# Modulation vectors from raw fp32 weight blocks held stationary, with silu(c) as the moving operand

## What is computed

```python
shift, scale, gate = jnp.split(jax.nn.silu(c) @ wm + bm, 3, axis=-1)        # wm: 2048 x 6144
shift_c, scale_c = jnp.split(jax.nn.silu(c_ctx) @ wm[:, :2 * D_MODEL] + bm[:2 * D_MODEL], 2, axis=-1)
hx = rmsnorm(h, norm_g[layer]) * (1.0 + scale[:, None]) + shift[:, None]
hc = rmsnorm(ctx, norm_g[layer]) * (1.0 + scale_c) + shift_c
proj = hx @ wi                                                              # queries, keys, values, gates of two attentions
...
oa = diff_attention(qa, ka, va, ka_c, va_c, ...)                            # attention "a"
ob = neighbourhood_attention(qb, kb, vb, kb_c, vb_c, rpb_l, rows)           # attention "b"
mixed = jnp.concatenate([oa, ob], axis=-1) @ w_out[layer]
h = h + gate[:, None] * mixed
return rmsnorm(h, final_g)
```

## Time and profile before

| | us |
|---|---|
| median of 3 runs | 3143.16 (3136.03 to 3157.03) |
| the profiled execution, its own time | 3152.64 |
| span of its trace | 3150.9 |
| first stage, start of the span to the first matmul of the projection a | 223.5 |
| attend_a, from its first POOL instruction to the first slab of projection b | 507.1 to 600.8 |
| projection b, queries and the first head of keys | 600.8 to 659.9 |

### The profile page before, as it was taken

One profiled execution on the slowest core, in us unless ns is written; L12 is line 12 of the kernel. 1 busy time (PEld: TensorE's weight loads), 2 busy tenths in 40 slices (PEclk: granted clock), 3 DMA queues, 4 the chain that ended last, 5 costly groups with the idle time before them and its releaser, 6 DMA issues. The chain is left out here.

```text
span 3150.9 us, 52606 instructions
## 1 busy us (share of the span) xinstructions
PE 2911.8 (92%) x15816; PEld 2475.9 (79%) x15816; DVE 1801.5 (57%) x3346; ACT 1450.7 (46%) x2697; POOL 621.6 (20%) x488
## 2 busy tenths in 40 slices
PE   6879997799979699987799999999999999999996
PEld 4658785688857599965699998888888888888885
DVE  5784325532345665455678785555555666666666
ACT  6663234432344344443344445555554555555553
POOL 0030001210000000000000077878761211111110
PEclk9999998899989899986999999999999999999998
DMA  6873237332424255442454577777776666666663
GB/s 237 287 232 131 89 105 289 87 122 94 144 82 170 103 186 184 165 155 87 153 186 168 177 183 175 186 187 187 187 193 238 216 218 220 217 214 217 220 212 133
DMA packets 182877, 554.08 MB, mean 176 GB/s; under 512 B 53664, under 2 KB 53696, under 8 KB 179488
## 3 DMA queue, kind: packets, MB, share of 16 engines
q1 hardware_dynamic: 137696, 517.03, 48.8%
q0 software_dynamic: 44544, 32.10, 5.9%
q10 hardware_dynamic: 576, 4.19, 0.3%
HBM read 532.13 MB, written 21.10 MB: 176 GB/s over the span
## 5 line engine op out<-in xcount | busy, mean ns | idle before, releaser
L153 DVE TENSOR_TENSOR w_lo<-raw,w_hi 128x512 fp32r<-128x512 f32 x1888 | 1306.0, 717 | 934.2 <-ACT w_hi L146 918.3
L146 ACT ACTIVATE w_hi<-raw 128x512 fp32r<-128x512 f32 x1888 | 1143.1, 629 | 938.7 <-PE PS L164 845.8
L1745 PE MATMUL PS<-h,w_hi 128*128 128x512 f32 x1504 | 533.1, 400 | 2.0 <-DVE w_lo L153 2.0
L1658 POOL DMA_INDIRECT g_dram<-gt,spot x256 | 414.2, 1618 | 458.4 <-DVE gt L1986 348.7
L1747 PE MATMUL PS<-h,w_lo 128*128 128x256 f32 x1504 | 423.1, 281 | 0.0
L162 PE MATMUL PS<-w_hi,wj_hi 128*128 128x512 f32 x1024 | 399.2, 390 | 4.9 <-DVE wj_lo L1794 4.9
L163 PE MATMUL PS<-w_lo,wj_hi 128*128 128x512 f32 x1024 | 398.8, 389 | 0.0
L164 PE MATMUL PS<-w_hi,wj_lo 128*128 128x512 f32 x1024 | 398.8, 389 | 0.0
L1745 PEld LDWEIGHTS PS<-h,w_hi 128*128 128x128 f32 x1504 | 283.4, 188 | 73.2 <-DVE w_lo L153 2.4
L1747 PEld LDWEIGHTS PS<-h,w_lo 128*128 128x128 f32 x1504 | 284.8, 189 | 0.0
L162 PE MATMUL PS<-h,w_hi 128*128 128x256 f32 x800 | 228.8, 286 | 5.0 <-DVE w_lo L153 2.9
(11 more groups left out here) (327 smaller groups left out, 4418.6 us busy)
## 6 DMA issues: line engine op xcount, KB each, us to landing
raw<-in_u_s SPq DMA_DIRECT2D x256, 512.0 KB
raw<-in_v SPq DMA_DIRECT2D x256, 512.0 KB
raw<-in_w_in_s SPq DMA_DIRECT2D x112, 512.0 KB
raw<-in_w_mod_s SPq DMA_DIRECT2D x96, 512.0 KB
raw<-in_w_in_a SPq DMA_DIRECT2D x64, 512.0 KB
raw<-in_w_in_b SPq DMA_DIRECT2D x64, 512.0 KB
raw<-in_w_out_s SPq DMA_DIRECT2D x64, 512.0 KB
g_dram<-h_buf SPq DMA_DIRECT2D x1, 16384.0 KB, 42.8
```

What stands on the lines that cost most here:

```text
L146: act.activation(w_hi[m % 2][:, half], raw[:, m % NRAW, half], ACT.Copy).then_inc(hi_ready, 1)
L153: dve.tensor_tensor(w_lo[m % 2][:, half], raw[:, m % NRAW, half], w_hi[m % 2][:, half].bitcast(F), ALU.subtract).then_inc(lo_ready, 1)
L1658: pool.indirect_dma_start(g_dram, bass.IndirectOffsetOnAxis(spot[:, t, h, k:k + 1], 0), gt[:, t, h, k:k + 1], None, compute_op=ALU.add).th ...
L1745: pe.matmul(PS[:, 6 + j % 2, :], w_hi[m % 2][:, c], h_both[:, kk, :, :].rearrange("p a t -> p (a t)"), start=(kk == 0), stop=False)
```

## The change

shift and scale are now made block by block of 128 features (k = 0 to 15). A slab of w_mod_s holds 8 blocks of 128x128 of w_mod, and two slabs (`half`) hold the 16 input blocks of one output block. Each 128x128 block of `raw`, in plain fp32 and neither rounded nor split, is the stationary side of one matmul with csilu (2 columns: c and c_ctx) as the moving side; 16 of these add up into two columns of PSUM, in which the result already lies as a column, so that mod_row and its transposes are gone. PE itself counts the slab as used (`lo_ready` by 2). Slabs 0 to 15 come before the transposes of x, 16 to 63 after them, and then 32 slabs of the gate (`w_gate_s`) in the same form. DVE adds the bias, makes the factor and applies both to xT for each k; ACT rounds and POOL subtracts as before. The counters that ACT, DVE and PE no longer raise one by one are raised once at the start.

Beside that, clearing h_buf and writing it over g_dram moves from attend_a (POOL, SP) into projection b, on POOL's queue: after the bias loads and ahead of the mask, as 8 DMAs of 2 MB. And attend_a transposes into one PSUM bank where it had two.

```diff
-N_MOD, N_WIN_A, N_WIN_B, ... = 96, 64, 64, ...
+N_MOD, N_WIN_A, N_GATE, N_WIN_B, ... = 64, 64, 32, 64, ...
 (sync, first stage)
                         load_slabs(sp, src_mod, 0, NRAW, N_MOD)
+                        load_slabs(sp, src_gate, base["gate"], 0, NRAW)
+                        load_slabs(sp, src_gate, base["gate"], NRAW, N_GATE)
                         load_slabs(sp, src_a, base["a"], 0, NRAW)
 (scalar)
-                        act.activation(cc_hi[:, :, :], cc[...], ACT.Copy).then_inc(cc_round, 1)
-                        round_slab(act, None, 0)
...
-                                round_slab(act, None, 8 * u + g + 1)
...
+                        act.sem_inc(hi_ready, 2 * (N_MOD + N_GATE))
+                        for t in range(4):
+                            act.wait_ge(x_in[t], 16)
...
+                        for k in range(KT):
+                            if k == KT - 1:
+                                round_slab(act, None, base["a"])
+                            act.wait_ge(affine, k + 1)
+                            act.activation(x_hi[:, k, :], xT[:, k, :], ACT.Copy).then_inc(x_round, 1)
 (vector)
-                            for g in range(16):
-                                split_slab(dve, q * 16, 16 + g + 1)
-                            for u in range(2):
-                                add_bias(q, 2 + u)
...
+                        for k in range(KT):
+                            dve.wait_ge(lo_ready, 8 * (k + 1))
+                            i = dve.tensor_tensor(mk[:, k, :, :], PS[:, 4 + k % 4, 0:4].rearrange("p (a w) -> p a w", a=2),
+                                                  biases[:, k, :][:, :, None].broadcast_to([P, 2, 2]), ALU.add)
+                            i.then_inc(mod_out, 1)
...
+                            for w in range(2):
+                                part = xT[:, k, w * T:(w + 1) * T]
+                                i = dve.tensor_scalar(part, part, ab[:, k, w:w + 1], mk[:, k, 0, w:w + 1], ALU.mult, ALU.add)
+                            i.then_inc(affine, 1)
+                        dve.wait_ge(lo_ready, 2 * base["a"])
+                        dve.tensor_tensor(gateT[:, :, :], PS[:, 1, 0:2 * KT]..., ALU.add)
+                        split_slab(dve, None, base["a"])
 (tensor)
-                                        mm3(pe, PS[:, 6 + u, :], (cc_hi[:, kk, :], cc_lo[:, kk, :]),
-                                            (w_hi[m % 2][:, c], w_lo[m % 2][:, c]), kk == 0, kk == KT - 1).then_inc(multiplied, 1)
...
+                        def shift_and_scale(k):
+                            if k >= 4:
+                                pe.wait_ge(mod_out, k - 3)
+                            for a in range(2):
+                                for half in range(2):
+                                    m = 4 * k + 2 * a + half
+                                    raw_wait(pe, (None, m))
+                                    for j in range(8):
+                                        last = pe.matmul(PS[:, 4 + k % 4, 2 * a:2 * a + 2], raw[:, m % NRAW, j * P:(j + 1) * P],
+                                                         csilu[:, 8 * half + j, :], start=(half == 0 and j == 0),
+                                                         stop=(half == 1 and j == 7))
+                                    last.then_inc(lo_ready, 2)
+                        for k in range(4):
+                            shift_and_scale(k)
                         pe.wait_ge(small, 64)
-                        mod_transposes(None, 0)
                         for k in range(KT):
...
                                 last = pe.transpose(PS[:, k % 4, t * P:(t + 1) * P], xs[:, t, k * P:(k + 1) * P], ident)
-                        with loop(pe, 5) as q:
-                            mod_pair(q, 1)
-                            mod_transposes(q, 1)
+                        for k in range(4, KT):
+                            shift_and_scale(k)
+                        pe.wait_ge(tr_outv, KT // 2)
+                        for e in range(KT):
+                            for half in range(2):
+                                m = base["gate"] + 2 * e + half
+                                raw_wait(pe, (None, m))
+                                for j in range(8):
+                                    last = pe.matmul(PS[:, 1, 2 * e:2 * e + 2], raw[:, m % NRAW, j * P:(j + 1) * P], ...)
+                                last.then_inc(lo_ready, 2)
 (attend_a)
-                        sp.wait_ge(blank, 1)
-                        sp.dma_start(g_blank, h_buf[...].broadcast_to([P, 8, TT * D])).then_inc(g_blanked, 16)
...
-                        pool.memset(h_buf[:, :, :], 0.0).then_inc(blank, 1)
...
-                                last = pe.transpose(PS[:, 4 + t, c * P:(c + 1) * P], at_[:, t, c * P:(c + 1) * P], ident)
+                                last = pe.transpose(PS[:, 4, c * P:(c + 1) * P], at_[:, t, c * P:(c + 1) * P], ident)
 (projection b, gpsimd)
                             pool.wait_ge(bias_in, 64)
+                            pool.memset(h_buf[:, :, :], 0.0).then_inc(blank, 1)
+                            pool.wait_ge(blank, 1)
+                            for c in range(8):
+                                pool.dma_start(g_blank[:, c, :], h_buf[...]).then_inc(g_blanked, 16)
```

More of the change, by code:

```diff
@@ L237, in peer_block_kernel @@
         at = 0
-        for name, n in (("mod", N_MOD), ("a", N_WIN_A), ("b", N_WIN_B), ("out", N_OUT), ("in2", N_WIN2),
+        for name, n in (("mod", N_MOD), ("gate", N_GATE), ("a", N_WIN_A), ("b", N_WIN_B), ("out", N_OUT), ("in2", N_WIN2),
                         ("out2", N_OUT2), ("wq", N_WQ), ("u", N_U), ("v", N_V)):
@@ L441, in _ @@
                         dve.wait_ge(small, 64)
-                        for u in range(2):
-                            add_bias(None, u)
                         for k in range(1, KT, 2):
@@ L500, in mod_transposes @@
-                        def mod_transposes(reg, pair):
-                            for u in range(2):
-                                tile = 2 * pair + u
-                                pe.wait_ge(row_in, tile + 1 if reg is None else reg * 2 + (tile + 1))
-                                if pair:
-                                    pe.wait_ge(mod_out, tile - 1 if reg is None else reg * 2 + (tile - 1))
-                                for c in range(4):
-                                    last = pe.transpose(PS[:, 4 + u, c * P:(c + 1) * P], mod_row[:, u, c * P:(c + 1) * P], ident)
-                                last.then_inc(mod_tr, 1)
-                                pe.wait_ge(mod_tr, tile + 1 if reg is None else reg * 2 + (tile + 1))
-                                pe.sem_inc(row_free, 1)
@@ L523, in _ @@
                             last.then_inc(tr, 1)
[L524 to L526 removed]
+                        for k in range(4, KT):
[6 more added lines that the diff above has]
+                                for j in range(8):
+                                    last = pe.matmul(PS[:, 1, 2 * e:2 * e + 2], raw[:, m % NRAW, j * P:(j + 1) * P],
+                                                     csilu[:, 8 * half + j, :], start=(half == 0 and j == 0),
+                                                     stop=(half == 1 and j == 7))
+                                last.then_inc(lo_ready, 2)
             def project(half_name, q_sb, k_sb, v_sb, g_sb, rope, nxt, ph, more_loads):
```

141 lines of the change are left out of this document (31 added, 110 removed).

## The result

| | before | after |
|---|---|---|
| median | 3139.6 us (4 runs, 3135.8 to 3157.0) | 3296.1 us (4 runs, 3290.5 to 3301.5) |
| ratio, 95% interval | | 1.0487 [1.0442, 1.0532] |
| span of the trace | 3150.9 | 3299.4 |
| first matmul of projection a | 223.5 | 355.6 |
| attend_a, first POOL instruction to first slab of projection b | 94.2 us | 91.8 us |

What follows compares the result with a forecast made beforehand. PE was taken to bound the kernel. First stage +131, attend_a -3.5 and projection b +10 make +137.5 us, added to the median 3143.2: 3281 us, 4.4% slower, range 3258 to 3318.

Steps and rivals of the forecast that it cites:

- The bound: Whole kernel: PE has work for 92% of the span, no other engine over 57%, so PE's gain or loss decides.
- Two loads a call, 0.2135 us a pair, clock down for the whole stage: First stage: 16 load-and-multiply pairs a slab, 1536 in all, at 1.2 GHz; 3.42 us a slab.
- The stage's sum: First stage up to projection a's start: 354.3 us where it was 223.5, so +131 us.
- the 1.7 us for a clock still high behind the transposes: First stage, 80 slabs behind the transposes: 1.7 us off their 273.3, for some 3.4 us of high clock.
- the clock stays up: Rival, first stage: pairs at 0.111 us, 1.78 a slab, stage 23.6 us earlier than before, 3126 us in all; chance 0.09.
- goes up and down: Rival, first stage: clock half the time at each level, 2.6 us a slab, +54.5, 3204 us in all; chance 0.05.
- The rival of a load that doesn't follow the clock: First stage: weights load at one rate of 0.11 us whatever the clock's level, 3126 us in all; chance 0.02.
- attend_a, -3.5: Start of attend_a: without the clearing of h_buf (3.54 us) ahead of the copies, PE's first scores start 3.5 us earlier.
- Projection b, +10: Projection b: the 16 MB of writes slow the slabs through the DMA queues; 10 us, with 0 and 26 as ends.
- the pace of slabs beside rows of 8 KB: Projection b: slabs 5.3 us each from 625.6 on, as seen beside x and ctx; slab 17 some 5 us late.
- shares by row length: Projection b: rows of 16 KB against the slabs' 4 give 6.7 us a slab until about 679; PE 15 late.
- The upper bound, 9.5 us a slab: Projection b: if slabs fare worse still beside the writes, 9.5 us each, the cost is 26 us.

## Why the prediction was right, step by step

**The bound.** Right. PE set the time; 258 us less of DVE's and ACT's work bought nothing.

**Two loads a call, 0.2135 us a pair, clock down for the whole stage.** Right. From 80.42 to the last load's end at 353.36 the 1280 loads take 0.2132 each. Both runs that halve one factor (128 columns, half of the calls) shorten the stage by 149 and 156 us. The prediction leaned on ten microseconds of another stage, in fp32r with 32 and 16 columns, and carried them over to some 280 us in plain fp32 with 2. The price of a load at the lower level was read from rows and held. That the clock would stay down for so long was the part that rows could not vouch for, and here the forecast was also fortunate.

**The stage's sum.** 354.3 forecast, 355.6 measured: transposes from 68.04 (68.2 forecast) to 77.92 (77.5), the wait for the bias addition to 80.42 (80.1). What was off is the 1.7 us for a clock still high behind the transposes, of which the first 768 loads show 0.4. The clock did rise within the transposes, as the forecast had it: 11 loads in 2 us up to 74, 19 in 2 us from there on, 9.9 us for the 64 where 9.3 was forecast. It was down again by 82. The rivals in which the clock stays up or goes up and down fell at the granted clock of 0.50.

**The rival of a load that doesn't follow the clock.** Fell: 212 ns at one level and 111 at the other, and both paces within the run with 128 columns.

**attend_a, -3.5.** The scores start that much earlier after POOL's first instruction (1.58 us against 5.03), but the stage is only 2.5 us shorter. Two other pairs of traces differ by the zeroing alone: on the old first stage 94.2 against 92.3, 1.9 us, and on the new one, with the zeroing put back, 96.1 against 91.8, 4.3. The term of 3.5 lies between them. The sign is right, and single traces can't tell its size better than to some 1 us.

**Projection b, +10.** The mechanism is right and this is the term that was mis-sized: it measured +16.9 in the trace, and 13.6 to 19.4 in the three others that have the same writes and no long split (72.6 to 78.5 us to the first key head, against 59.1). The forecast had ACT waiting some 10 us for slabs, and it waited 37.6. I had two values, the pace of slabs beside rows of 8 KB (5 us late) and shares by row length (6.7 us a slab, 15 late), and took a value between them. The measured pace is 6.23 us for as long as the writes run, so the second was the right one (it had reckoned with 392 GB/s for both streams, and 424 flowed), and the row that spoke for the first had rows half as long. The upper bound, 9.5 us a slab, stands on no row, and nothing like it was seen. The run with 2 KB rows and the one on ACT's queue show the share by row length. The Trainium skill, DMA: Bandwidth & Descriptors, section "Queues, rings and completion order", has each DMA engine take turns between its queues a packet at a time; the slabs' pace here agrees, in that the queue with longer rows got more of the time.

**The total.** 3281 forecast, 3296 measured, inside the range. The terms of the sum lack 11 us (stage +1, projection a +2.6, attend_a +1, projection b +7), and between the two profiled executions it is just these 11: 3290 forecast, 3301.5 measured. The other 4 come from the step to medians: the profiled execution before was 9.5 us above its median, the one after 5.3. Projection a's 2.6 were in no step. They are no accident of one trace: from its first matmul to the start of attend_a all eleven traces with the new first stage take 284.9 to 286.3 us, and the three with the old one 283.1, 283.0 and 284.0. The cause stays open, as no run was made on it.

## What to carry to other kernels

Price a step that becomes many small matmuls by the nearest run in the same trace with a stationary block of the same size and as few moving columns, and read the granted clock of that stretch before its duration: here it doubled the price of a load. When a bulk write moves into a stage that streams, compute the stream's share from the row lengths of both, and look at what each issuing engine has to do behind its issues. When one trace is all there is for a small term, say so: projection b's first key head came 72.6 to 83.2 us behind the first slab in five traces of the same zeroing. Relieving an engine is worth nothing while another sets the end.

## What the runs showed that was not expected

- Moving 64 times as many columns made the kernel 145 us faster: 3151.1 us with 128 columns, 3296.1 with 2 and 3297.2 with 64. With the same loads, the granted clock from 120 to 160 us was 1.00, 0.50 and 0.50.
- Eight DMA issues of 2 MB held ACT's queue for 40.4 us in rows of 2 KB and for 10.0 us in rows of 16 KB; they held POOL for 7.0 and 4.3.
- One DVE subtraction of 0.69 us lasted 10.51 us in two traces with rows of 2 KB and 10.16 in one with 16 KB, each time beside POOL's additions right behind its DMA issues. Four traces with the same order have none, nor has any in which the additions stand elsewhere.
